# Decode attention: where ACT and DVE split the value pages, moved from page g-2 ahead of key page g to page g behind it

## What is computed

```python
k_past = cache_k[l][page_table].reshape(n_dec, PAST_LEN, DA_HEADS, 2 * DA_HEAD_DIM)
v_past = cache_v[l][page_table].reshape(n_dec, PAST_LEN, DA_HEADS, DA_V_DIM)
k_all = jnp.concatenate([k_past, ka], axis=1);  v_all = jnp.concatenate([v_past, va], axis=1)
s = q . k / sqrt(64) - slope * distance, masked     # two maps per head
p = softmax(s);  a = p[:, :, 0] - lam * p[:, :, 1];  o = a @ v_all
```

## Time and profile before

| | us |
|---|---|
| median of 3 runs | 1933.44 (1932.71 to 1934.54) |
| profiled execution | 1933.36 |
| its span, first to last instruction | 1931.1 |
| PE busy | 1776.0 (92% of the span) |
| DVE busy | 780.2 (40%) |
| ACT busy | 661.2 (34%) |
| POOL busy | 97.2 (5%) |

### The profile page before, as it was taken

The page is one execution under the profiler, slowest core; times in us unless marked ns, Lnnn a source line. Parts: engine busy times, 40 slices in busy tenths (PEclk is TensorE's granted clock), DMA queues, the critical chain, the costliest instruction groups (busy, mean ns, idle before and its releaser), DMA issues.

```text
span 1931.1 us, 32243 instructions
## 1 busy us (share of the span) xinstructions
PE 1776.0 (92%) x13095; PEld 1678.0 (87%) x13095; DVE 780.2 (40%) x1084; ACT 661.2 (34%) x867; POOL 97.2 (5%) x169
## 2 busy tenths in 40 slices
PE   5999999998998775989889999899999899999996
PEld 5999999987997545777768999779998799999996
DVE  2333332244223775776753222344344433333123
ACT  3333331124223554666753222123322433332111
POOL 0000000000002420000000000210000000000002
PEclk9999999999998898999989999999999999999998
DMA  4222222230430014787851232152222122222221
GB/s 140 88 88 88 89 88 93 82 101 30 134 124 33 1 39 147 260 281 269 278 178 45 86 102 85 46 184 88 88 87 87 34 89 88 88 88 84 85 98 46
DMA packets 146734, 204.09 MB, mean 106 GB/s; under 512 B 5538, under 2 KB 127330, under 8 KB 146658
## 3 DMA queue, kind: packets, MB, share of 16 engines
q1 hardware_dynamic: 145506, 198.55, 31.6%
q0 software_dynamic: 1152, 4.46, 0.6%
HBM read 191.59 MB, written 11.40 MB: 105 GB/s over the span
## 4 chain that ended last, share of the span: by engine, by line
PE 85%; DVE 6%; ACT 5%; issue 3%; DMA 0%; SPq 0%; POOL 0%; POOLq 0%; ACTq 0%; DVEq 0%
PE ps L297 68%; PE ps L1255 3%; PE ps L1280 2%; PE ps L1237 2%; PE ps L974 2%; DVE vp_lo L1377 2%; ACT vp_hi L1373 1%; PE ps L988 1%; ACT kt_hi L1355 1%; PE ps L614 1%; PE ps L1683 1%; PE ps L1675 1%; PE ps L1295 1%; PE ps L699 1%; DVE kt_lo L1356 1%
## 5 line engine op out<-in xcount | busy, mean ns | idle before, releaser
L297 PE MATMUL ps<-xh,w_hi_t 128*128 128x272 f32 x2432 | 512.1, 292 | 27.4 <-DVE xl L651 18.6
L297 PE MATMUL ps<-xl,w_hi_t 128*128 128x272 f32 x2432 | 506.4, 290 | 0.0
L297 PE MATMUL ps<-xh,w_lo_t 128*128 128x272 f32 x2432 | 505.8, 290 | 0.0
L283 DVE TENSOR_TENSOR w_lo_t<-w_raw,w_hi_t 128x2048 fp32r<-128x2048 f32 (+1 forms) x112 | 252.4, 2254 | 519.2 <-ACT w_hi_t L279 519.2
L297 PEld LDWEIGHTS ps<-xh,w_hi_t 128*128 128x128 f32 x2432 | 385.6, 191 | 32.5 <-issue 21.1
L297 PEld LDWEIGHTS ps<-xl,w_hi_t 128*128 128x128 f32 x2432 | 386.7, 191 | 0.0
L297 PEld LDWEIGHTS ps<-xh,w_lo_t 128*128 128x128 f32 x2432 | 384.6, 191 | 0.0
L279 ACT CAST w_hi_t<-w_raw 128x2048 fp32r<-128x2048 f32 (+1 forms) x112 | 209.9, 1874 | 277.5 <-PE ps L297 277.5
L297 PE MATMUL ps<-hh,w_hi_t 128*128 128x272 f32 x704 | 145.8, 288 | 0.0
L297 PE MATMUL ps<-hl,w_hi_t 128*128 128x272 f32 x704 | 145.3, 288 | 0.0
L297 PE MATMUL ps<-hh,w_lo_t 128*128 128x272 f32 x704 | 144.9, 287 | 0.0
(11 more groups left out here) (243 smaller groups left out, 2040.4 us busy)
## 6 DMA issues: line engine op xcount, KB each, us to landing
w_raw<-in_ffn_w_gu_dram SPq DMA_DIRECT2D x44, 1024.0 KB, 5.0
w_raw<-in_w_in_dram SPq DMA_DIRECT2D x32, 1024.0 KB, 5.6
k_page<-in_cache_k_dram SPq DMA_DIRECT2D x64, 512.0 KB, 4.2
v_page<-in_cache_v_dram SPq DMA_DIRECT2D x64, 512.0 KB, 4.7
w_raw<-in_ffn_w_down_dram SPq DMA_DIRECT2D x16, 1024.0 KB, 5.1
w_raw<-in_ffn_w_down_dram SPq DMA_DIRECT2D x8, 768.0 KB, 4.4
w_raw<-in_w_branch_a_dram SPq DMA_DIRECT2D x4, 1024.0 KB, 5.1
st_in<-in_state_ret_dram SPq DMA_DIRECT2D x8, 512.0 KB, 5.3
```

Of the source, the lines that this page charges most:

```text
L283: nc.vector.tensor_tensor(w_lo_t[:, j, 0:nk], w_raw[:, j, 0:nk], w_hi_t[:, j, 0:nk].bitcast(F32), ALU.subtract).then_inc(lo_split, 1)
L297: mm = nc.tensor.matmul(ps[:, bank + half, 0:HALF], w[:, j, k, w_cols], m[:, k0 + k, half * HALF:half * HALF + HALF], start=start and k == ...
```

## The change

On ACT, value pages 2 and 3 are split together behind key 3, and from page 4 on value g comes directly behind key g. `act_keep` is moved from ahead of key 2 to behind it. On DVE the values are moved in the same way, and `dve_weigh` comes behind value 5 in place of key 5. No instruction is added or removed, and the lists of TensorE, POOL and SP stay as they are. The new order on ACT: low score rows, key 0, exponential, key 1, value 0, key 2, keep, p, value 1, key 3, value 2, value 3, key 4, value 4, key 5, value 5, key 6, value 6, key 7, value 7.

```diff
@@ act_step
                     self.act_value(act, b - 1, 0)
+                self.act_key(act, b, 2)
                 if older:
                     self.act_keep(act, b - 2)
-                self.act_key(act, b, 2)
                 if past:
                     self.act_p(act, b - 1)
                     self.act_value(act, b - 1, 1)
                 self.act_key(act, b, 3)
+                if past:
+                    self.act_value(act, b - 1, 2)
+                    self.act_value(act, b - 1, 3)
                 for g in range(4, PAGES):
+                    self.act_key(act, b, g)
                     if past:
-                        self.act_value(act, b - 1, g - 2)
-                    self.act_key(act, b, g)
-                if past:
-                    self.act_value(act, b - 1, 6)
-                    self.act_value(act, b - 1, 7)
+                        self.act_value(act, b - 1, g)
@@ dve_step
                 self.dve_key(dve, b, 3)
+                if past:
+                    self.dve_value(dve, b - 1, 2)
+                    self.dve_value(dve, b - 1, 3)
                 for g in range(4, PAGES):
+                    self.dve_key(dve, b, g)
                     if past:
-                        self.dve_value(dve, b - 1, g - 2)
-                    self.dve_key(dve, b, g)
-                    if past and g == 5:
-                        self.dve_weigh(dve, b - 1)
-                if past:
-                    self.dve_value(dve, b - 1, 6)
-                    self.dve_value(dve, b - 1, 7)
+                        self.dve_value(dve, b - 1, g)
+                        if g == 5:
+                            self.dve_weigh(dve, b - 1)
```

## The result

The changed kernel takes 1938.75 us (median of 7 runs, 1938.29 to 1940.64) against 1933.55 before (7 runs): the ratio is 1.0028, 95% interval 1.0018 to 1.0037, so it is slower by 5.2 us, with 3.5 to 7.2 by the interval. One run of the kernel before on that occasion, 4430.40 us, stands apart from all others and is counted nowhere. The profiled execution took 1940.64 us.

What follows compares the result with a forecast made beforehand. TensorE was taken to bound the kernel (85% of the span), so ACT and DVE edits count only where it waits. Delays of 2.8 + 2.9 + 1.2 = 6.9 us on 1933.36 gave 1940.3 us, range 1935.4 to 1944.4.

Steps and rivals of the forecast that it cites:

- The link: Pages 4 and 5: value 4 waits for `values` 2 on ACT, so key 5 and score pair 2 come 0.40 us later.
- Pair 3: Pages 6 and 7: value 6 waits for `values` 4, so key 7 and score pair 3 come 0.41 us later.
- The gain of nothing: TensorE: `values` 3 can run about 0.9 us earlier, but the score pair behind it waits for key 5: gain 0.
- Rival A: TensorE ahead of `values` 3 and 5: the wait goes, nothing replaces it; 9.9 us faster, 1923.5 us; chance 0.06.
- Keep: ACT: key 2 must wait for turn 2, idling 0.42 us; score pair 1 comes 0.2 us later in 6 steps.
- the loads: SP: lists of loads unchanged, value places free earlier or at the same time: 0.
- Rival C: Value pages have not landed when split; if all loads were the slowest, 2.8 us more, 1943.1 us; chance 0.07.
- the signs that the prediction named against itself: Key 5 leaving DVE no later than before, value splits waiting for their loads, or the clock below 1.00 inside steps.
- rival D: TensorE's longer pauses drop the clock to the 1.2 GHz level in score pairs: some 19 us, 1960 us; chance 0.03.
- The sum: Over the decode steps: 7 x 0.40 + 7 x 0.41 + 6 x 0.2 = 6.9 us slower, 1940.3 us in all.

Runs made afterwards that it cites:

- the two runs with the third place: Three places for `vp_hi` instead of two, ACT's wait eased and a second wait on DVE: on the changed kernel 1937.85 us, on the kernel before 1944.82 us.

## Why the prediction was right

**The link** held as it was worked out. Value 4 waits for `values` 2 and starts 0.10 us after its modelled end (0.09 expected). Counted from turn 4, key 5 starts on DVE after 4.32 us in place of 3.92 and score pair 2 opens after 5.65 in place of 5.26: 0.39, forecast 0.40. Pair 3, from turn 6: 5.61 in place of 5.22, 0.39, forecast 0.41. That it is ACT's wait which does this, the two runs with the third place show. The rows of TensorE from which these are counted, beside those shown above: turns 4 and 6 and the opening of pair 3 before, turn 6 after.

```profile
845.72 1.07 PE L1237 MATMUL ps<-ident,k_page 128*128 128x128 f32 x8
...
853.09 1.04 PE L1237 MATMUL ps<-ident,k_page 128*128 128x128 f32 x8
...
858.31 0.39 PE L1252 MATMUL ps<-bias_r,ident_r 128*128 128x260 f32 x1
```

```profile
856.77 1.04 PE L1237 MATMUL ps<-ident,k_page 128*128 128x128 f32 x8
```

**The gain of nothing.** `values` 3 did come 0.97 us earlier, and TensorE stood 1.38 us in front of the score pair in place of it. Rival A, in which the wait of `values` goes and nothing replaces it, is refuted. Its sign was possible, though: the two runs that leave the place ahead of key 5 empty are faster.

**Keep** was put at 0.2 us a step; the run that moved only keep gave 0.16. The prediction gave 0.42 us both as ACT's wait for turn 2 and as the delay of what follows. These are two things: the wait is 0.34, since keep had started 0.10 ahead of the end of value 0, and the delay, 2.69 to 3.13 us from turn 2 to value 1, is 0.44.

**Step 1** is where a part was missed: the sum put the loads at nothing. Rival C was judged by step 3, where page 4 is wanted 6.1 us after its issue. In step 1 there is no `merge`, and the load is issued 2.3 us ahead of turn 4, where step 3 of the changed kernel has 4.2. SP issued value pages 4 and 5 there from 783.02:

```profile
783.02 1.57 SPq L1152 DMA_DIRECT2D v_page<-in_cache_v_dram  x2
```

and ACT stood for page 4 until 787.77, 4.75 us behind, the ordinary time to landing of the earlier trace rows:

```profile
787.77 1.05 ACT L1373 CAST vp_hi<-v_page 128x1024 fp32r<-128x1024 f32 x1 [0.68 <-DMA v_page<-in_cache_v_dram]
```

Step 1 cost 1.26 us in place of 0.81. So C was true of one step in seven and false of the other six, and of the signs that the prediction named against itself, a value split that waits for its load, one came.

**The clock** (rival D) stayed at the 2.4 GHz level through steps 2 to 7, the answer to the earlier trace rows:

```profile
781.00:993.00 212.00, 182.17 (x1274) 155.40 (x1273) 145.70 (x213) 133.88 (x197) 8.26 (x42) 1.00 0.78 260
...
846.00:876.00 30.00, 25.60 (x185) 22.11 (x184) 20.59 (x31) 18.68 (x29) 1.38 (x7) 1.00 0.79 269
```

TensorE's pauses of 1.38 us, twice a step, are longer than any in the same steps of the kernel before, where the longest is 1.27. The rule of the Trainium skill, TensorE: Matmul & The Clock Gate, section "A second HAM failure mode: psum-queue depth-cycling", by which frequent short idles make the clock swing, does not agree with these steps, where the granted clock was 1.00 throughout. Step 1 is another matter, in both kernels: the prediction's 1.00 was read between 836 and 866 us, while its own row at 0.50, from 776 to 778, lies in step 1. That stretch at the 1.2 GHz level is 6.8 us long before the change and after it, so the difference does not come from it. Before, then after:

```profile
773.00:779.00 6.00, 6.00 (x32) 5.71 (x31) 4.75 (x7) 3.11 (x6) 0.00 (x0) 0.50 0.75 246
...
774.00:780.00 6.00, 6.00 (x32) 5.71 (x31) 4.63 (x7) 2.98 (x6) 0.00 (x0) 0.50 0.76 235
```

**The sum.** Forecast were 6.9 us for the steps and 1940.3 us in all; the profiles give 7.09 and 7.14 for the steps, and the medians are 1938.75 and 1940.43. Some 0.4 us of the steps is the load in step 1. Without it the score pairs and keep come to some 6.7, a shade less than forecast: two small misses of opposite sign. The medians moved by 5.2 and 7.0 us. What lies between 5.2 and 7.1 is not explained by the steps; the stretches around them differ by as much between executions, and whether the first median shows more than that stays open.

## What to carry to other kernels

On an engine that runs its list in order, the place of an instruction has a price in what waits behind it: an early value page is worth nothing if the one that takes its old place must wait for a result that the same step has just begun to compute, and the path runs through the instruction behind that. When a wait is removed, look at the next wait on the same engine and ask what feeds it before counting the gain; here both hung on DVE, and the distance between two key splits there set the opening of the score pair. And check a load's lead in the first turn of a pipeline apart from the steady one.

## What was not expected of the hardware

A second semaphore wait in front of a DVE instruction, on a semaphore that had been reached long before, cost 0.07 us, and 0.11 us in each step of the kernel before. In each of the two kernels with it there are 31 cases in which DVE stood waiting for the hi part. The lo part started 0.10 us after the hi part's end in all of them but the one late case, against 0.03 in every such case of the other kernels; the other semaphore had been reached 0.7 us or more ahead. Why it costs this is not shown.
